# Prologue by quarters: 8 modulation loads for 4 chunks ahead of the first unit, and 3 loads of weights mixed into each 8 that follow

## The reference

```python
mod = silu(c) @ w_ada + b_ada                  # c: 2048; w_ada: 2048 x 12288
sh1, sc1, gt1, sh2, sc2, gt2 = split(mod, 6)
h = rms_norm(x, g_norm1) * (1 + sc1) + sh1     # 256 x 2048
proj = h @ w_in                                # 2048 x 3904
```

## Time and profile before

| | |
|---|---|
| median of 3 runs | 2698.8 us (2695.52 to 2700.94) |
| the profiled execution's own time | 2699.22 us |
| its span in the trace | 2697.4 us |
| PE busy | 2615.0 us, 97% |
| DVE, ACT busy | 59%, 43% |
| HBM read | 556.31 MB, 208 GB/s over the span |

### The profile page before, as it was taken

The page is one execution under the profiler, slowest core; times in us unless marked ns, Lnnn a source line. Parts: engine busy times, 40 slices in busy tenths (PEclk is TensorE's granted clock), DMA queues, the critical chain, the costliest instruction groups (busy, mean ns, idle before and its releaser), DMA issues.

```text
span 2697.4 us, 32987 instructions
## 1 busy us (share of the span) xinstructions
PE 2615.0 (97%) x12162; PEld 2083.3 (77%) x12162; DVE 1583.7 (59%) x1755; ACT 1163.8 (43%) x1514; POOL 52.8 (2%) x84
## 2 busy tenths in 40 slices
PE   6999879989999999999999999999999999999997
PEld 2667656778888888887888877888888888888886
DVE  1467665657777555557755454556556565656565
ACT  2344444444333444443544455444444444444443
POOL 1010010000000000000000000000000000000000
PEclk9999989989999999999999999999999999999999
DMA  9967766647777655555655544665655555555552
GB/s 390 378 229 261 271 233 231 217 137 250 248 245 245 195 187 187 188 190 188 214 188 184 175 141 145 200 209 203 208 191 187 191 191 192 187 187 187 190 190 103
DMA packets 262819, 561.74 MB, mean 208 GB/s; under 512 B 9186, under 2 KB 13492, under 8 KB 261836
## 3 DMA queue, kind: packets, MB, share of 16 engines
q1 hardware_dynamic: 260688, 549.25, 60.4%
q0 software_dynamic: 1664, 9.19, 1.0%
q10 hardware_dynamic: 380, 2.13, 0.2%
HBM read 556.31 MB, written 4.21 MB: 208 GB/s over the span
## 4 chain that ended last, share of the span: by engine, by line
PE 91%; DVE 4%; DMA 2%; ACT 1%; issue 1%; POOL 0%; DVEq 0%; SPq 0%; POOLq 0%; ACTq 0%
PE acc L628 83%; PE bank L712 2%; PE bank L658 2%; DMA early_mix<-in_w_ada 2%; DVE w_lo L1645 1%; PE bank L862 1%; ACT w_hi L1133 0%; PE acc L853 0%; PE acc L1062 0%; PE acc L852 0%; PE acc L1061 0%; PE bank L724 0%; PE bank L686 0%; ACT probs L1340 0%; PE bank L676 0%
## 5 line engine op out<-in xcount | busy, mean ns | idle before, releaser
L1645 DVE TENSOR_TENSOR w_lo<-raw,w_hi 128x1024 fp32r<-128x1024 f32 x852 | 1037.9, 1225 | 816.3 <-ACT w_hi L1133 784.5
L1133 ACT ACTIVATE w_hi<-raw 128x1024 fp32r<-128x1024 f32 x852 | 901.3, 1060 | 1061.3 <-PE acc L628 960.7
L628 PE MATMUL acc<-w_hi,actT_hi 128*128 128x512 f32 (+1 forms) x2112 | 834.7, 395 | 1.2 <-DVE actT_lo L1783 0.8
L628 PE MATMUL acc<-w_hi,actT_lo 128*128 128x512 f32 (+1 forms) x2112 | 821.7, 389 | 0.0
L628 PE MATMUL acc<-w_lo,actT_hi 128*128 128x512 f32 (+1 forms) x2112 | 821.5, 389 | 0.0
L628 PE MATMUL acc<-w_hi,mixT_hi 128*128 128x512 f32 (+1 forms) x1280 | 503.5, 393 | 8.5 <-DVE mixT_lo L1773 5.4
L628 PE MATMUL acc<-w_hi,mixT_lo 128*128 128x512 f32 (+1 forms) x1280 | 498.0, 389 | 0.0
L628 PE MATMUL acc<-w_lo,mixT_hi 128*128 128x512 f32 (+1 forms) x1280 | 497.2, 388 | 0.0
L628 PEld LDWEIGHTS acc<-w_hi,actT_hi 128*128 128x128 f32 x2112 | 397.9, 188 | 115.0 <-issue 25.8
L628 PEld LDWEIGHTS acc<-w_hi,actT_lo 128*128 128x128 f32 x2112 | 397.8, 188 | 83.0
L628 PEld LDWEIGHTS acc<-w_lo,actT_hi 128*128 128x128 f32 x2112 | 398.3, 189 | 79.0 <-issue 1.0
(11 more groups left out here) (270 smaller groups left out, 1128.6 us busy)
## 6 DMA issues: line engine op xcount, KB each, us to landing
raw<-in_w_ff SPq DMA_DIRECT2D x128, 1024.0 KB, 5.1
raw<-in_w_in SPq DMA_DIRECT2D x108, 1024.0 KB, 5.1
raw<-in_w_ada SPq DMA_DIRECT2D x64, 1024.0 KB, 5.0
raw<-in_w_gate SPq DMA_DIRECT2D x44, 1024.0 KB, 5.1
raw<-in_w_up SPq DMA_DIRECT2D x44, 1024.0 KB, 5.1
raw<-in_w_down SPq DMA_DIRECT2D x44, 1024.0 KB, 5.0
early_mix<-in_w_ada SPq DMA_DIRECT2D x16, 1024.0 KB, 9.5
wide<-in_w_ada SPq DMA_DIRECT2D x16, 1024.0 KB, 8.8
```

What stands on the lines that cost most here:

```text
L628: last_mm = pe.matmul(acc[p][:, t, 0:width], act[x][:, k0 + c, t * P:(t + 1) * P], w[:, u % SPL, c * NW:c * NW + width], start=first and c ...
L1133: act.activation(w_hi[:, u % SPL, :], raw[:, ld % RAW, (u % DU) * 1024:(u % DU + 1) * 1024], ACT.Copy) \
L1645: dve.tensor_tensor(w_lo[:, u % SPL, :], raw[:, ld % RAW, (u % DU) * 1024:(u % DU + 1) * 1024], w_hi[:, u % SPL, :].bitcast(F32), ALU.subt ...
```

## The change

The segments become four of four chunks. The lead is then 8 loads (sh1 and sc1 for chunks 0 to 3). The three weight loads of a quarter have 3, 3 and 2 early loads behind them instead of 2 each. The parts stand in slots 0 to 3 of each six units: one, two, two and three of them (EARLY_AT), for the first three quarters. In the prologue, gains and second rows come behind a3, and the steps "x" begin behind a4. Columns, modulated(0), two splits, modulated(1) and the third split are now steps of prologue(), between the last x steps. No parts stand between the lead and the first unit. On the DVE the modulation of a quarter moves from the slot behind that of its columns to the same slot, as on ACT. The number of loads, parts, units and splits stays; four groups of four chunks take the place of two groups of eight.

```diff
--- before.py
+++ after.py
@@ -59,10 +59,12 @@
 
 
 
-SEGMENTS = ((0, 8), (8, 4), (12, 4))
+SEGMENTS = ((0, 4), (4, 4), (8, 4), (12, 4))
 LEAD = 2 * SEGMENTS[0][1]
 NPRO = 32
 PRO_RING = 4
+EARLY_GAPS = (3, 3, 2)
+EARLY_AT = (1, 2, 2, 3, 0, 0)
 GAPS = [0] * 12 + [1] * 16 + [2] * 9 + [1] * 14 + [0] * 3
 ORDER = "".join("w" + "a" * g for g in GAPS)
 assert len(GAPS) == 54 and sum(GAPS) == 80 - NPRO
@@ -111,14 +113,12 @@
         steps.append(("part", a))
         if a >= 1:
             steps += [("columns", n) for n in completed(a - 1)]
-        if 5 <= a < 13:
-            steps.append(("x", 2 * (a - 5)))
-        if a == 13:
-            steps.append(("gains",))
-        if a == 14:
-            steps.append(("rows",))
-    steps += [("columns", n) for n in completed(LEAD - 1)]
-    return steps + [("part", LEAD), ("part", LEAD + 1)]
+        if a == 3:
+            steps += [("gains",), ("rows",)]
+        if a >= 4:
+            steps.append(("x", 2 * (a - 4)))
+    steps += [("x", 8), ("columns", 1), ("modulated", 0), ("split",), ("split",), ("x", 10), ("modulated", 1)]
+    return steps + [("x", 12), ("x", 14), ("split",)]
 
 
 def modulation(u):
@@ -133,7 +133,10 @@
 
     def early(v):
 
-        return [LEAD + 1 + v] if 0 < v < NPRO - LEAD - 1 else []
+        if not 0 <= v < 18:
+            return []
+        first = LEAD + v // 6 * 8 + sum(EARLY_AT[:v % 6])
+        return list(range(first, first + EARLY_AT[v % 6]))
     events = [("row", n) for a in products(u - 3) for n in completed(a) if n >= len(GROUPS)]
     events += [("columns", n) for a in products(u - 2) for n in completed(a)]
     events += [("columns", n) for a in early(u - 1) for n in completed(a)]
@@ -451,7 +454,7 @@
                 sp.dma_start(dst, view).then_inc(raw_in[k % RAW], 16)
                 n[0] += 1
                 if kind == "w":
-                    for _ in range(2):
+                    for _ in range(EARLY_GAPS[(ORDER[:n[0]].count("w") - 1) % 3]):
                         if asked[0] < NPRO:
                             early_ada()
                     while ORDER[n[0]:n[0] + 1] == "a":
@@ -1254,17 +1257,10 @@
             skip_banks(2)
             todo_of = {"columns": lambda n_: skip_banks(1), "gains": lambda: skip_banks(2), "rows": lambda: skip_banks(1),
                        "x": lambda k: bank_to(xT[:, k:k + 2, :].rearrange("p k s -> p (k s)")),
-                       "part": lambda a: skip_banks(takes_bank("part", a))}
+                       "part": lambda a: skip_banks(takes_bank("part", a)), "modulated": modulated, "split": split}
             for s in prologue():
                 if s[0] in todo_of:
                     todo_of[s[0]](*s[1:])
-            for _ in range(DU):
-                split()
-            modulated(0)
-            for _ in range(AHEAD - DU):
-                split()
-            for q in pieces_of(1)[1:]:
-                modulated(q)
 
             def qk_sums(g):
                 sum_ready()
@@ -1905,17 +1901,10 @@
                 bias_fills.append((L.n["bank"] % 2, L.n["bank"] // 2 + 1))
                 L.n["bank"] += 1
             todo_of = {"part": part_sums, "columns": part_columns, "diagonal": lambda: diagonal(inv_rms()),
-                       "x": lambda k: turned(), "gains": gain_columns, "rows": second_rows}
+                       "x": lambda k: turned(), "gains": gain_columns, "rows": second_rows, "modulated": modulated, "split": split}
             for s in prologue():
                 if s[0] in todo_of:
                     todo_of[s[0]](*s[1:])
-            for _ in range(DU):
-                split()
-            modulated(0)
-            for _ in range(AHEAD - DU):
-                split()
-            for q in pieces_of(1)[1:]:
-                modulated(q)
 
             def head_weight():
 
@@ -2087,7 +2076,7 @@
 
             for u in range(24):
                 unit(window(u - 24))
-                for q in modulated_at(u - 1):
+                for q in modulated_at(u):
                     modulated(q)
                 if u == 14:
                     head_weight()
```

## The result

The changed kernel takes 2731.45 us (median of 4 runs, 2730.83 to 2732.59), beside 2699.16 for the kernel before (4 runs, 2695.52 to 2700.94): a ratio of 1.0123, 95% interval 1.0108 to 1.0138, or 32.3 us slower. The forecast was 2720, 21.2 us slower, with a range that ended at 2730. The direction was right, and so was the mechanism of the quarters; three terms around it were sized too small, and the time came out above the range.

What follows compares the result with a forecast made beforehand. The PE, busy 97% of the span, was taken as the bound. The first mirror chunk 19.9 us later plus 1.35 of slow matmuls, summed as 21.2, on 2699.2 gave 2720 us; range 2708 to 2730.

Steps and rivals of the forecast that it cites:

- Part 1, the lead: Prologue with a lead of 8 loads: first unit starts at 43.3 us, 18.7 earlier, an offer and not yet a gain.
- the PE's row from the gains on: Prologue, PE steps after a3: gains 1.8 us, second rows to 26.0, then parts, x steps and columns to 37.7.
- the excess of the first unit (0.65): First unit: half the extra time the first two units take now, 0.65 us, charged to it.
- Part 2, the quarter: Quarters: SP waits for the DVE's copy behind the second weight load's splits; period 34.8 us, 0.5 added for slow matmuls.
- The half step on the modulation's slot: Quarters, DVE: modulation one slot earlier delays only the split of w4, whose landing hides it; no cost.
- Part 3, the mirror: First mirror chunk: bias load waits for the last copy, takes 7.2 us; chunk at 152.9 against 133.0, 19.9 later.
- w12 is nearly in by then: Mirror: reason for taking the bias load as alone in flight, at 7.2 us.
- The forecast's upper bound, 4: Mirror: 4 us more if the bias load shares, as x does with the first loads.
- the 1 to 2 us estimated from it: Mirror: engines taking packets from queues in turn would make the bias load pay 1 to 2 us for w12.
- Behind the mirror: After the mirror: nothing gives the loss back, since the PE is the chain there too; no further term.
- Rival C: Whole kernel: clock falls in gaps and stays low, 2 x 3 us, bias load shares, 4; +31, 2730; chance 0.11.
- Rival A: Whole kernel: copies come in time, quarters at 28.4 us, mirror at 131.0 to 135.0; no difference, 2697 to 2701; chance 0.08.

Runs made afterwards that it cites:

- experiment 1: Changed kernel with the DVE's columns and sum copies ahead of the split of their slot in slots 0 to 15; 2720.00 us.
- experiment 2: Changed kernel with 2, 3 and 3 early loads behind a quarter's three weight loads in place of 3, 3 and 2; 2720.59 us.
- experiment 5: Changed kernel with the PE, not the DVE's copy, handing back the last early buffer of each group to SP; 2722.78 us.
- experiment 9: Changed kernel with six buffers for the early loads in place of four, nothing else; 2706.23 us.
- experiment 3: Changed kernel with SP holding weight load w10 and what follows back until the bias load has landed; 2728.22 us.
- experiment 4: Changed kernel with gains and second rows moved from behind a3 to the end of the prologue; 2733.43 us.
- experiment 10: Changed kernel with the six mirror chunks two slots later, nothing else; 2724.68 us.
- Experiment 7: Changed kernel with the DVE's part of the modulation put back one slot later, where it was before the change; 2747.09 us.
- experiment 11: Changed kernel with six early-load buffers and the mirror chunks two slots later, no other edits; 2697.01 us.
- the control: Kernel before the change with the mirror chunks two slots later, nothing else; 2700.06 us, ratio 1.0004.
- experiment 6: Changed kernel with the PE handing early buffers back and the DVE's copies ahead of the split of their slot; 2715.77 us.

## Why the prediction was right in kind and 11 us short

Three steps of the sum failed: the PE's row of the lead, worked out with durations at the full clock (the first unit came 3.5 us later), the bias load, taken as alone in flight (4.0 us), and the rest behind the mirror, put at nothing (2.4 us). The quarters, where the loss was expected, came as forecast.

**Part 1, the lead.** Forecast: first unit at 43.3 us. It came at 46.81. The step that failed is the PE's row from the gains on: it took matmul durations from places where the clock was at full speed. In the changed kernel it stood at 0.50 from 21 to 34 us, and the gains took 3.38 us and not 1.78, the columns 1.87 and not 1.02, the first x step 2.05 and not 1.16: 3.5 us up to the first unit. That the excess of the first unit (0.65) was not needed took 0.9 off, and a13 and w2 landed 9.0 us after a9's part and not 7.7 put 1.3 on: w2 at 63.57, forecast 59.7, 3.9 late.

**Part 2, the quarter.** Forecast: SP waits for the DVE's copy behind the second split of w2, and a period of 34.8 us, 35.3 with slow matmuls. Measured: 34.9 twice. Between landings the sum of steps held to some tenths (w2 to copy 4.1, forecast 4.2; a21's issue to w5's landing 98.48 - 90.87 = 7.6, forecast 5.1 + 2.6). The DMA share from 45 to 140 us was 0.83, forecast 0.8. Experiments 1, 2, 5 and 9 each take away one link of the chain (order on the DVE, order on SP, owner of the buffer, length of the ring) and each gives back part of the loss or nearly all of it; that is what shows the mechanism. The totals mix this with the clock of the prologue; the quarters show it by themselves. With the chain left as it was they took 34.9 or 35.0 us (the changed kernel and experiment 3) and up to 37.8 (4 and 10), with a link gone 32.3 and 32.5 (1), 33.2 and 31.0 (2), 33.7 and 32.1 (5), 28.8 and 28.2 (9).

Two loads at an empty queue: the Trainium skill's figure ("DMA: Bandwidth & Descriptors", section "Anatomy of one DMA", which gives it for DMAs that GpSimd issues, where these are SP's) would have given 2.0 us plus 2.1 MB over 436 GB/s, an estimate of 6.8. In the trace it took 7.5 to 7.7 us from the issue of the first to the landing of the second, all five times in the quarters, as the prediction's own 5.1 + 2.6 has it.

The half step on the modulation's slot ("hides it", so nothing) was wrong in kind, though not in the sum: I asked what the earlier place costs and never what the old place would have cost in the new pattern. Experiment 7 measured it, 15.6 us.

**Part 3, the mirror.** Forecast: the bias load alone, 7.2 us. It took 11.15, and experiment 3 shows that SP's loads beside it made the difference. The sentence that failed is "w12 is nearly in by then". By the prediction's own spacing w9 lands at T3+2.6, so w12 at T3+10.3, 4.2 us behind POOL's issue at T3+6.1 (in the trace 4.1: 152.9 against 148.84), and the next load went out at 149.94. "As it is now" was wrong as well: before, w12 alone stood beside the bias load, issued at 121.14 and in at 127.5, 2.8 us behind POOL's issue at 124.72. The forecast's upper bound, 4, is what came. The Trainium skill's rule (same page, section "Queues, rings and completion order": each DMA engine takes packets from its queues in turn) agrees in kind with 11.2 beside 7.2; the 1 to 2 us estimated from it assumed one load in flight where there were three (w11, w12 and the one behind). The slow matmuls behind it cost 2.2 us and not 1.35: the second chunk was 29.25 late, the first 27.0.

**Behind the mirror** the forecast put the rest at nothing. The distance stays at 29.25 us for 150 us more and then grows by 2.4. Most of it comes at one place, where the PE is not idle longer but slower. The chain after, and then the same steps before:

```profile
314.19 1.85 PE bank L661 x8
316.05 3.75 PE acc L631 x12
```

```profile
284.96 1.06 PE bank L658 x8
286.02 2.98 PE acc L628 x12
```

That is 1.6 us of the 2.4; the rest comes in steps of 0.1 to 0.4 by 430 us. In both kernels this stretch begins behind the same idle time of the PE (1.22 and 1.23 us). That the clock fell there in one kernel and not in the other is seen, its cause is not. No experiment was made on it.

**The sum.** 21.2 forecast, plus 3.1 for w2 and the periods (3.9 less 0.8), 4.0 for the bias load, 0.9 for the slow unit, 2.4 behind: 31.6, the growth of the span. The forecast's own range ended at +29, with the first unit 2 us later, the bias load shared and each quarter 1.0 longer. The first two came, the first of them at 3.5 and not 2; the third did not, and the 2.4 behind the mirror stood in no bound. Rival C (the clock and the shared load: +31, with a chance of 0.11) has nearly the measured total and the shared load, but it put 6 us of the clock into quarters that stayed at 34.9; that its total fits is luck. The shared load does not come from late copies: in experiments 9 and 11, where nobody waits for them, the bias load took 10.4 and 12.1 us. Rival A (no difference) is what experiment 9 made of the kernel, with the mirror at 134.8 us as A said (131 to 135) and the time, 2706, above A's 2697 to 2701.

## What to carry to other kernels

Before a load order is changed, write down for each load whose release it waits for and what stands ahead of that release on the other engine: a wait that is free with the queue full costs its whole length once the queue is at its end. The cure that gave most was neither a better order nor another owner but two more buffers, 25 of 32 us; they ended two waits of SP's at once, the one for the copy and the one ahead of a12. And price a moved step at both places in the new pattern, not only at the new one.

## What the runs showed of the hardware

- A load of 1.5 MB on POOL's queue took 7.2 us in experiment 3 with nothing beside it, 7.2 in the kernel before with the end of one load of 1 MB of SP's beside it, 7.0 in the control, and 10.4 to 12.1 us in the other eleven kernels; in the kernel after, three loads of SP's stood beside it.
- The clock in the prologue was not the same from kernel to kernel with the same instructions up to there: the gains took 3.38 us after, 1.78 in experiments 1, 5 and 6, 2.55 in 2, 3.37 in 3 and 7, 3.38 in 10, and the first unit's first matmul started between 42.5 and 47.0 us. So its start in one of these traces told that in another only to within 4.5 us.
- In experiment 3 the row of the granted clock reads 1.00 from 14 to 38 us, while up to 34 us parts last 1.94 us and the gains 3.37, as they do at 0.50 elsewhere. In the kernel before, too, parts last 1.93 us up to 23 us where that row reads 1.00. There the durations say more than the row.
- In the kernel after, the PE stood 4.64 us ahead of the columns at 67.83, and its clock was at 0.50 from 66 to 74 us; it was so again at 104 to 108 and 138 to 142, one quarter and two later.
